# Building PEER gate matrices in DRAM by indirect accumulate DMAs instead of one-hot products on TensorE

## What is computed

```python
q = (xb @ w_q).reshape(PEER_BLOCK, PEER_HEADS, 2, PEER_QDIM // 2)      # 8 heads, 2 x 128
s = einsum('thpd,hpkd->thpk', q, subkeys)                              # 128 keys per half
s1, i1 = top_k(s[:, :, 0], 16);  s2, i2 = top_k(s[:, :, 1], 16)
cand = s1[..., :, None] + s2[..., None, :]                             # 256 candidates
sc, pos = top_k(cand, 16);  idx = (i1 * 128 + i2) taken at pos
g = softmax(sc)
act = gelu(einsum('thkd,td->thk', u[idx], xb))                         # u, v: 16384 x 1024
out = einsum('thk,thkd->td', g * act, v[idx])
```

## Time and profile before

| | |
|---|---|
| median of 3 runs | 3716.45 us (3703.6 to 3716.63) |
| span of the profiled execution | 3700.4 us |
| PE busy | 3558.4 us, 96% |
| VectorE busy | 2666.9 us, 72% |
| ScalarE busy | 2003.8 us, 54% |
| GpSimd busy | 139.6 us, 4% |
| DMA queues | 568.38 MB, mean 154 GB/s, q1 49.0% of 16 engines |
| median of runs less span | 16 us |

### The profile page before, as it was taken

One profiled execution on the slowest core, in us unless ns is written; L12 is line 12 of the kernel. 1 busy time (PEld: TensorE's weight loads), 2 busy tenths in 40 slices (PEclk: granted clock), 3 DMA queues, 4 the chain that ended last, 5 costly groups with the idle time before them and its releaser, 6 DMA issues.

```text
span 3700.4 us, 61292 instructions
## 1 busy us (share of the span) xinstructions
PE 3558.4 (96%) x22710; PEld 3113.8 (84%) x22710; DVE 2666.9 (72%) x5607; ACT 2003.8 (54%) x3922; POOL 139.6 (4%) x134
## 2 busy tenths in 40 slices
PE   7999999999998999999999999999899999979999
PEld 5877787888887899999998888888698888878888
DVE  5447733699868688888767776774765899686666
ACT  3345522566668555555557544434454666684444
POOL 0002000000012000000002000000100000030000
PEclk9999999999999999999999999999999999999999
DMA  5213222455645566566655566633044566605665
GB/s 206 82 67 138 94 97 83 144 183 182 186 151 159 167 187 184 185 186 184 187 184 152 161 186 198 195 119 111 9 164 136 176 187 182 187 29 165 188 190 172
DMA packets 142313, 568.38 MB, mean 154 GB/s; under 512 B 15920, under 2 KB 17456, under 8 KB 130352
## 3 DMA queue, kind: packets, MB, share of 16 engines
q1 hardware_dynamic: 142128, 566.16, 49.0%
HBM read 565.05 MB, written 1.05 MB: 153 GB/s over the span
## 4 chain that ended last, share of the span: by engine, by line
PE 82%; DVE 12%; ACT 3%; issue 2%; DMA 1%; POOL 1%; SPq 0%; DVEq 0%; POOLq 0%; ACTq 0%
PE ps L584 52%; PE ps L1081 13%; PE ps L1099 10%; PE ps L1083 6%; DVE low L1835 3%; DVE arena L1835 3%; ACT arena L1283 2%; DMA ring<-wmod_in 1%; POOL arena L2619 1%; DVE hot_found L1835 1%; DVE arena L2387 1%; DVE arena L2378 1%; DVE ring_low L1835 0%; DVE arena L2380 0%; DVE arena L2375 0%
## 5 line engine op out<-in xcount | busy, mean ns | idle before, releaser
L1283 ACT ACTIVATE high<-ring 128x512 fp32r<-128x512 f32 x1632 | 1028.4, 632 | 1014.7 <-PE ps L584 502.2
L1835 DVE TENSOR_TENSOR low<-ring,high 128x512 fp32r<-128x512 f32 x1632 | 1078.1, 690 | 290.4 <-ACT high L1283 279.4
L584 PE MATMUL ps<-h_pair,high 128*128 128x512 f32 x3456 | 1236.7, 398 | 17.6 <-DVE h_pair L1835 10.3
L584 PE MATMUL ps<-h_pair,low 128*128 128x256 f32 x3456 | 979.7, 283 | 0.0
L584 PEld LDWEIGHTS ps<-h_pair,high 128*128 128x128 f32 x3456 | 653.6, 189 | 171.1 <-issue 11.9
L1081 PE MATMUL ps<-wt,high 128*128 128x512 f32 x2016 | 706.3, 397 | 5.7 <-DVE low L1835 5.7
L584 PEld LDWEIGHTS ps<-h_pair,low 128*128 128x128 f32 x3456 | 655.0, 190 | 0.0
L1083 PE MATMUL ps<-wt,low 128*128 128x256 f32 x2016 | 562.4, 279 | 0.0
L1283 ACT ACTIVATE arena<-ps 128x256 f32<-128x256 f32 (+2 forms) x659 | 274.8, 427 | 382.3 <-PE ps L584 334.0
L1081 PEld LDWEIGHTS ps<-wt,high 128*128 128x128 f32 x2016 | 379.1, 188 | 97.2 <-issue 3.0
L584 PE MATMUL ps<-arena 128*128 128x128 f32 (+7 forms) x2536 | 355.1, 311 | 56.5 <-ACT arena L1283 44.2
(11 more groups left out here) (202 smaller groups left out, 4296.5 us busy)
## 6 DMA issues: line engine op xcount, KB each, us to landing
ring<-u_in SPq DMA_DIRECT2D x384, 512.0 KB, 3.6
ring<-v_in SPq DMA_DIRECT2D x384, 512.0 KB, 3.6
ring<-win_in SPq DMA_DIRECT2D x54, 1024.0 KB, 4.9
ring<-wmod_in SPq DMA_DIRECT2D x24, 1024.0 KB, 5.0
ring<-wq_in SPq DMA_DIRECT2D x48, 512.0 KB, 3.6
ring<-wmod_in SPq DMA_DIRECT2D x48, 512.0 KB, 3.7
ring<-wbr_in SPq DMA_DIRECT2D x16, 768.0 KB, 4.3
ring<-wout_in SPq DMA_DIRECT2D x8, 1024.0 KB, 4.9
```

The source lines that it names most:

```text
L584: return pe.matmul(o, l_, r, start=first, stop=last)
L1283: return act.activation(o, i_, f, **kw_)
L1835: return dve.tensor_tensor(o, a, b, op)
```

## The change

The one-hot arrays, `route`, `route_copy`, `gate_products` and `gate_mult` go. Three DRAM tensors `gates` of 16384 x 256 float32 (16.8 MB each, one for each pass) take their place. SyncE's queue fills each with zeros in 64 parts of 256 KB, between the weight loads: `gates[0]` beside w 4 to 15 and u 0 to 51 of pass (0, 0), `gates[1]` beside u 64 to 127 of that pass, `gates[2]` beside v 0 to 63 at layer 0's end. `rank` turns the picks into cell numbers, and GpSimd issues 128 indirect DMAs for each half of the tokens, each adding 128 single floats (one for each token) to DRAM. Before picks 16, 32, ... 112, the first of each head after the first head, it waits until the DMAs so far have landed. `gate_chunk` loads 128 KB of gates for each chunk of v into a ring of three, the first one after all DMAs of the pass, and `weigh` multiplies A by them.

What lay between the groups is moved: `rows_between` keeps only the modulation rows and the context sums. The next pass's norm goes beside u chunks 108 to 127, and its `modulated` and first two w chunks (`hi`, `lo`) beside the modulation rows. `key_scores` has a new wait on `mod_read`.

```diff
@@ SyncE's queue
+            def zero_part(i, n):
+                if n == 0 and i == 0:
+                    sp.wait_ge(*at("zero"))
+                some = slice(n * CHUNKS // ZERO_PARTS, (n + 1) * CHUNKS // ZERO_PARTS)
+                sp.dma_start(gates[i].rearrange("(p c) (a b) -> p (c a) b", p=P, b=P)
+                             [:, 2 * some.start:2 * some.stop, :],
+                             zero.unsqueeze(1).broadcast_to([P, 2 * (some.stop - some.start), P])
+                             ).then_inc(*inc(f"zeroed{i}", n, by=16))
+            def gate_chunk(pp, c):
+                v, i = VN["v", pp, c], passes_before(pp)
+                if c == 0:
+                    sp.wait_ge(*at("gated", pp, 1, PICKS - 1))
+                if v >= 3:
+                    sp.wait_ge(cnt.sem("w_ready"), v - 2)
+                sp.dma_start(gate_ring[:, v % 3, :], gates[i].rearrange("(p c) t -> p c t", p=P)[:, c, :]
+                             ).then_inc(cnt.sem(f"gate_in{v % 3}"), 16)
...
                     for c in range(CHUNKS):
                         if before:
+                            gate_chunk(before, c)
                             chunk(("v", before, c))
                         chunk(("u", pp, c))
@@ TensorE: gate_products becomes rows_between
+                    pe.wait_ge(*at("psc_read", pp, 1, 3))
+                    if l + 1 == DEPTH:
+                        return
+                    for n in range(MOD_PASS):
+                        for hf in range(2):
+                            mod_half(pp, 2 * n + hf)
+                        if n:
+                            mod_turn(l + 1, pp[1] * MOD_PASS + n - 1, ps[7], modrow_g)
...
@@ VectorE: rank
-                                link(dve.tensor_reduce(sel[:, q, h0 * TOPK:(h0 + 4) * TOPK], eqm, AX.X, ALU.add))
+                                link(dve.tensor_reduce(pf[:, some, :].rearrange("p h k -> p (h k)"), eqm, AX.X, ALU.add))
                                 yield
+                        if passes_before(pp):
+                            dve.wait_ge(*at("gated", every_pass[passes_before(pp) - 1], 1, PICKS - 1))
+                        link(dve.scalar_tensor_tensor(out=pa, in0=pa, scalar=float(KEYS), in1=pb, op0=ALU.mult, op1=ALU.add))
+                        link(dve.tensor_scalar(pa, pa, float(SEQ), vec[:, 0, V_TOK + t:V_TOK + t + 1], ALU.mult, ALU.add))
+                        link(dve.tensor_copy(pick_cell[:, t, :], pa.rearrange("p h k -> p (h k)")))
@@ VectorE: weigh
+                    dve.wait_ge(cnt.sem(f"gate_in{v % 3}"), 16 * (v // 3 + 1))
+                    link(tt(A[:, c, :], A[:, c, :], gate_ring[:, v % 3, :], ALU.mult))
                     link(dve.tensor_scalar(wt[:, v % 2, 0, :], A[:, c, :], 1.0, None, ALU.mult))
@@ GpSimd
+                    pool.wait_ge(*at(f"zeroed{i}", ZERO_PARTS - 1))
+                    for t in range(2):
+                        pool.wait_ge(*at("sel", pp, t))
+                        for n in range(PICKS):
+                            if n % TOPK == 0 and n:
+                                pool.wait_ge(*at("gated", pp, t, n - 1))
+                            pool.indirect_dma_start(
+                                cells, bass.IndirectOffsetOnAxis(ap=pick_cell[:, t, n:n + 1], axis=0),
+                                pick_gate[:, t, n:n + 1], None, compute_op=ALU.add
+                            ).then_inc(*inc("gated", pp, t, n, by=16))
```

More of the change, by code:

```diff
@@ L329, in write_program @@
         modrow_g = flat[:, 6 * D:6 * D + 512].rearrange("p (a b) -> p a b", b=256)
[L330 to L332 removed]
+        gate_ring = flat[:, 7 * D:7 * D + 3 * SEQ].rearrange("p (a b) -> p a b", b=SEQ)
+        gates = [nc.dram_tensor(f"gates{i_}", (KEYS * CHUNKS, SEQ), F32, kind="Internal").ap() for i_ in range(3)]
         rstd2 = flat[:, 7 * D + 3 * SEQ:8 * D]
@@ L551, in _ @@
                         sp.dma_start(early_raw[i], win_in[l + 1, i]).then_inc(*inc("early_in", i, by=16))
+                    gate_chunk(before, c)
                     chunk(("v", before, c))
+                    if l + 1 < DEPTH and c < ZERO_PARTS:
+                        zero_part(2, c)
             last = passes(DEPTH - 1)[-1]
@@ L1131, in key_scores @@
                         pe.wait_ge(*at("keys_in", pp))
+                        if before:
+                            pe.wait_ge(*at("mod_read", l + 1, before[1]))
                     pe.wait_ge(cnt.sem("u_read"), QN["w", pp, j] + 3)
@@ L1195, in mod_half, with rows_between @@
                     i.then_inc(cnt.sem("half_free"), 1)
-                def gate_products(pp, nxt, before):
+                def rows_between(pp, nxt):
                     pe.wait_ge(cnt.sem("u_read"), QN["u", pp, CHUNKS - 1] + 3)
[L1200 to L1215, removed]
-                                pe.wait_ge(*at("sq1", l + 1, 0, k))
[L1217 to L1226, removed]
@@ new lines, in rows_between @@
+                    pe.wait_ge(*at("psc_read", pp, 1, 3))
[6 more added lines that the diff above has]
+                            mod_turn(l + 1, pp[1] * MOD_PASS + n - 1, ps[7], modrow_g)
+                        if not nxt and n == MOD_PASS - 4:
+                            for k in range(KB):
+                                pe.wait_ge(*at("sq1", l + 1, 0, k))
+                                i = mm(ps[6][:, 0:SEQ], ones, h2T[:, k, :], k == 0, k == KB - 1)
+                            i.then_inc(*inc("ss1", l + 1, 0))
@@ L1261, in _ @@
                             one_in(("u", pp, c))
[L1262 to L1268, removed]
+                        both_range(before, pp, 2, CHUNKS)
+                    rows_between(pp, nxt)
                     if before:
@@ L1725, in _ @@
                             modulated(pp, k)
+                    after = passes(l)[passes(l).index(pp) + 1:]
+                    nxt = after[0] if after else None
                     for j in range(WQ):
-                        if before or j >= 2:
+                        if j >= 2:
                             hi(("w", pp, j))
```

234 lines of the change are left out of this document (83 added, 151 removed).

## The result

The changed kernel takes 4730.1 us (median of 4 runs, 4729.4 to 4737.5) against 3710.6 us for the kernel before (median of 4 runs; the 3716 used in the forecast is the median of 3 of them): 1.275 times the time before, 95% interval 1.273 to 1.277. The forecast was 3818 us in a range of 3570 to 4450. The direction was right, the size was not, and the time lies outside the range.

A forecast was written before the change was run, and what follows sets the result against it. TensorE, busy 96% of the span, was taken to bound the kernel. Stalls 286 + refills 12 + weigh 7 - savings 203 = +102 us on the profiled 3700.4; with 16 us between median and span, 3818 us, range 3570 to 4450.

The forecast's parts named there:

- The stages saved: Gate stages of the three passes: 62 + 55 + 86 = 203 us saved, with modulation stages of 40 and 42 us left.
- The moved steps and weigh: Next norm beside u 108 to 127 at no cost; weigh's extra VectorE product in v adds 7 us, bounds 0 and 20.
- The zeros: Zero stores beside the weight stream: taken as 0 us, at the upper end 43 us.
- The windows: Time from ranked half 0 to the first gate load, for 256 DMAs a pass: 310, 484 and 228 us.
- The price c of one indirect DMA: GpSimd's scatter: 1.61 us for each DMA, built from neighbouring rows; bounds 0.42 and 3.5, break-even at 1.41.
- the forecast's own formula: Stall before v in each pass: what 256c exceeds the windows by; 102 + 0 + 184 = 286 us forecast.
- GpSimd's own work: Part of each scatter DMA's price: 1.06 us for 128 addresses, from a full GpSimd instruction that reads 128 partitions.
- Every DMA is paid whole: Rival for the scatter: if few can be in flight, each costs its landing, 1.9 to 3.5 us; 4514 to 5204; chance 0.09.
- Landing beside the streams: Scatter landings: waited for 7 times in 128 DMAs, 3.6 us each; 15 of 16 DMAs have no wait before them.
- Waits between heads: Part of each scatter DMA's price: 7 waits for a landing of 3.6 us on 128 DMAs, 0.20 us.
- VectorE's share: Part of each scatter DMA's price: half of a 0.69 us VectorE instruction that GpSimd may meet, 0.35 us.
- Faster at 0.36: Chance 0.36 that the whole kernel gets faster, for scatter DMAs below 1.38 us each; same 0.07, slower 0.57.

The follow-up runs named there:

- no_scatter: The changed kernel without its 768 indirect DMAs, zeros, gate loads and moved steps kept: 3523.9 us, 0.949 of the time before.
- zeros_later: The changed kernel with the second gate matrix's zeros moved to u 0 to 31 of pass (0, 1), two parts a chunk: 4692.9 us.
- alone_1024: No model: six stages of 48 indirect DMAs, ring of 1024 bytes; additions alone 2.51 us each, plain writes 1.49, each waiting for the one before 3.3.
- alone_16384: No model: the same six stages of 48 indirect DMAs with a ring of 16384 bytes; additions 1.86 us each, plain writes 1.29, each waiting 3.2.
- lock: No model: stages of 24 additions, ring of 1024 bytes, alone or beside 70 VectorE instructions; longest DMA_INDIRECT 24.0 us beside unbroken two-input subtractions.

## Why the prediction was wrong, step by step

**The stages saved** were right: forecast 203 us less 7, measured 187 by no_scatter. The modulation stages take 46 and 45 us (40 and 42 forecast), and the last stage vanished. The reason given for their length was right only in part. I let the loads alone bound them, over 400 GB/s; they ran at 295 and 247, because the queue waited for TensorE to free a slot for 34.7 of 46 us. TensorE's clock is 0.56 and 0.63 there, unlike 0.98 in the gate stage, and its 192 products take 596 ns each instead of 391. The first stage, 1086 to 1132:

```profile
SPq L509 <- PE ps L613: 34.7, 24, 2.8
L613 PE MATMUL ps<-ring,csil 128*32 128x256 f32 x192 | 23.5, 596 | 8.0 <-DMA ring<-wmod_in 6.7 <-DVE arena L1808 0.9
```

Loads and a slow TensorE wait for each other in turn; how much of the 6 and 3 us over the forecast is the clock's wasn't tested.

**The moved steps and weigh** cost about as forecast. VectorE's new product takes 0.426 us, and in 200 us of v alone of no_scatter it has 29.1 us of idle time before it, where 58.7 stood before the rounding, with 71 chunks done for 72 and TensorE busy for all of it.

**The zeros** didn't slow u: TensorE is busy 216 of 218 us at a DMA share of 0.98. The sum counted them against the stream alone. Their cost fell on the scatter, 37 us by the one run of zeros_later.

**The windows** were right: 310, 484 and 228 us forecast, 1187 - 862 = 325, 2408 - 1921 = 487 and 3886 - 3660 = 226 measured. So was the mechanism: SyncE's queue stands at `gate_chunk`.

**The price c of one indirect DMA is the step that failed.** Forecast 1.61 us; measured from first to last start of a pass's 256 (windows 600:1120 on, with 255 steps): (1626.6 - 862.2)/255 = 3.00, (2683.9 - 1921.0)/255 = 2.99 and (4354.9 - 3659.9)/255 = 2.73 us. Put into the forecast's own formula, 256 x 3.00 - 325 = 443, 256 x 2.99 - 487 = 278 and 256 x 2.73 - 226 = 473 us, against stalls of 448, 285 and 478. Its terms:
- GpSimd's own work: 1.06 taken from the earlier trace rows, an arithmetic instruction, which says nothing of what issuing a DMA costs. An addition takes 1.55 + 0.30 = 1.85 us. With this term alone corrected c would have been 2.4 us, inside the range but far off.
- Room in the ring: no term at all in the sum. It costs 2.51 - 1.86 = 0.65 us with nothing else running. `dynamic_dma_scratch_size=1024` stands in the kernel's last lines (three additions in a group with it, four with 1280, one with 512), and the rival *Every DMA is paid whole* named few DMAs in flight as a mechanism, but I gave it 0.09.
- Landing beside the streams: the sum charged a landing once in 16 DMAs, but GpSimd waits for one after every three at most, and beside loads it is later. So c is 4.0 us at a DMA share of 0.98, 3.2 at 0.69, 2.6 in the stalls at 0.18 to 0.20.
- Waits between heads, 0.20: 28 us of waiting over (1, 1), 0.11.
- VectorE's share, 0.35: no row or run shows that an indirect DMA waits for half a VectorE instruction. What the runs show in its place is 1.60 us an instruction in the changed kernel against 1.55 alone, 0.05.

The chances went wrong with it. Faster at 0.36 needed c under 1.38; a scatter of additions that never waited for the ring would still take 1.85 us, and no run shows additions at a shorter pitch. The range's upper end, c = 2.5 (4436 us by the forecast's formula, written as 4450), was set short of the bound of 3.5 that the rows gave, and the measured 2.7 to 3.0 lies between. The rival *Every DMA is paid whole* was the nearest, and not quite what happened: what is paid is one landing for each group of up to three, on top of GpSimd's own 1.85 us.

The runs show 3.3 us for additions that wait one for another (alone_1024; 3.2 in alone_16384), and no fixed price for those that don't. That VectorE holds a DMA_INDIRECT up shows in `lock` (24.0 us) and alone_1024 (96.4 us) and not in alone_16384, where the same additions beside the same subtractions took 1.55 us each. It doesn't decide this kernel: its longest of 768 is 3.4 us.

**No version of the scatter that was tried beats the kernel before.** One instruction here takes one cell for each partition, so a pass needs 256. At GpSimd's own 1.86 us these are 476 us against windows of 325, 487 and 226: even an endless ring would leave stalls of 151 and 250 us, more than the 187 that are gained. A mix, with the one-hot stage for half of the tokens, wasn't tried, nor was the whole kernel with a ring that never fills: the 151 and 250 are an estimate from alone_16384.

## What to carry to other kernels

Before costing DMAs that GpSimd issues, price three things apart: GpSimd's time for each instruction (here 1.85 us an addition and 1.27 a plain write, its 0.30 us between two included), how many fit into its ring (here three additions or seven plain writes with 1024 bytes), and the landing time beside the streams that share the engines (in alone_1024 5.1 us beside loads, 2.9 without). In these runs they don't overlap as one would hope: the pace comes out as the first plus one wait for each group, divided by the number in the group (2.25 us worked out and 2.27 measured with four, 3.5 and 3.53 with one). Plain writes show it best: a landing of 2.1 us and seven in flight would hide fully behind 1.27 us each, and yet the pace with 1024 bytes was 1.49. Work that must end at a fixed point has a window: count the instructions against it first, and if its last wait stands on the queue that loads everything else, each microsecond over is a microsecond of the whole kernel. Where a resource appears in no row of the profile, such as a ring no one used yet, keep the upper bound in the range.

## What the runs showed of the hardware that I had not expected

- The addition costs GpSimd itself 0.58 us more than a plain write of the same 128 cells: 1.55 against 0.97 us an instruction, apart from the ring. For the DMA engines it is 144 packets against 32.
- When the ring is full, GpSimd idles about as long with one addition on its way (1.8 to 2.1 us) as with four (1.8 to 2.2): it behaves as if the whole ring had to empty before it goes on.
- One DMA_INDIRECT can last until VectorE's work has ended (each long one ended 1.4 us after it): 96.4 and 106.6 us in alone_1024 (the second beside loads too) and 24.0 in lock, beside back-to-back subtractions from two SBUF tensors. With a ring of 16384 bytes the same 48 additions beside the same stream took 1.55 us each and 88.9 us in all. All three long ones came after a wait for room in a small ring; that the full ring is what exposes GpSimd to VectorE's work is an argument from these runs, not shown.
